# Loading the first modulation columns in two blocks and forming the first eight projection tiles in two halves

## What is computed

```python
c_act = jax.nn.silu(c)
mod = c_act @ w_ada[l] + b_ada[l]
shift1, scale1, gate1, shift2, scale2, gate2 = jnp.split(mod, N_MOD, axis=-1)
h = modulate(rms_norm(x, norm1_g[l]), shift1, scale1)
p = h @ w_in[l]
y_rwkv = rwkv7_mix(p[..., :RWKV_COLS], ...)
y_fox = fox_mix(p[..., RWKV_COLS:], ...)
y = jnp.concatenate([y_rwkv, y_fox], axis=-1) @ w_out[l]
x = x + gate1[:, None, :] * y
h = modulate(rms_norm(x, norm2_g[l]), shift2, scale2)
x = x + gate2[:, None, :] * moe_ffn(h, ...)
```

## Time and profile before

| what | value |
|---|---|
| median of 3 runs | 1242.16 us (1240.57 to 1243.15) |
| span of the profiled execution, first to last instruction | 1237.4 us |
| TensorE matmul, share of the span | 84% |
| VectorE, ScalarE, GpSimd | 26%, 15%, 9% |
| bytes moved | 455.85 MB, 368 GB/s over the span |

### The profile page before, as it was taken

One profiled execution on the slowest core, in us unless ns is written; L12 is line 12 of the kernel. 1 busy time (PEld: TensorE's weight loads), 2 busy tenths in 40 slices (PEclk: granted clock), 3 DMA queues, 4 the chain that ended last, 5 costly groups with the idle time before them and its releaser, 6 DMA issues.

```text
span 1237.4 us, 28436 instructions
## 1 busy us (share of the span) xinstructions
PE 1044.5 (84%) x11067; PEld 523.5 (42%) x11068; DVE 318.7 (26%) x886; ACT 185.3 (15%) x403; POOL 110.2 (9%) x225
## 2 busy tenths in 40 slices
PE   3999999999897999999999796969696969696665
PEld 1777876645342444444444342424242424242222
DVE  0266445448221222222222121212121202121112
ACT  2330224423110111111111010101010101010001
POOL 7020002040000000000000000000010000000000
PEclk9999999999898999999999998889897979898877
DMA  9952236898899939999999999999999999999996
GB/s 367 408 197 67 69 141 233 314 391 306 359 409 424 388 121 430 425 428 427 428 425 430 426 428 427 426 428 426 427 427 429 428 427 428 427 426 428 427 426 285
DMA packets 49521, 455.85 MB, mean 368 GB/s; under 512 B 4790, under 2 KB 5916, under 8 KB 17104
## 3 DMA queue, kind: packets, MB, share of 16 engines
q1 hardware_dynamic: 43152, 417.91, 81.3%
q10 hardware_dynamic: 4960, 33.09, 6.4%
q0 software_dynamic: 1376, 4.38, 1.1%
HBM read 454.29 MB, written 1.07 MB: 368 GB/s over the span
## 4 chain that ended last, share of the span: by engine, by line
PE 50%; DMA 32%; DVE 8%; SPq 4%; issue 2%; ACT 1%; another core or an unknown queue 0%; ACTq 0%; DVEq 0%; POOLq 0%; POOL 0%
DMA raw<-in_w_gate_up 26%; PE bank L2071 19%; PE bank L2085 9%; PE bank L1636 7%; DMA odd<-in_w_gate_up 4%; PE bank L2043 2%; PE bank L1962 2%; SPq L422 2%; PE bank L2094 2%; DMA raw<-in_w_in 1%; DVE aT L1532 1%; DVE gated L1517 1%; DVE ups L1521 1%; SPq L438 1%; DVE ups L1059 1%
## 5 line engine op out<-in xcount | busy, mean ns | idle before, releaser
L2071 PE MATMUL bank<-raw,xT 128*32 128x512 f32 x2176 | 282.2, 665 | 108.3 <-DMA raw<-in_w_gate_up 100.6
L2071 PEld LDWEIGHTS bank<-raw,xT 128*32 128x32 f32 x2176 | 74.6, 117 | 294.9 <-issue 169.3
L1517 DVE TENSOR_TENSOR gated<-bank,bias_i 128x256 f32<-128x256 f32 x51 | 21.6, 424 | 592.9 <-PE bank L2094 592.9
L2085 PE MATMUL bank<-raw,aT 128*32 128x256 f32 x2448 | 142.3, 380 | 10.4 <-DVE aT L1532 10.4
L2071 PE MATMUL bank<-odd,xT 128*32 128x512 f32 x1088 | 131.5, 634 | 20.4 <-DMA odd<-in_w_gate_up 20.3
L962 ACT ACTIVATE evg<-bank 128x512 f32<-128x512 f32 x51 | 30.5, 597 | 689.2 <-PE bank L2071 688.9
L685 POOL TENSOR_TENSOR gatehot<-onehot,gates 128x128 f32<-128x128 f32 x102 | 54.7, 555 | 871.0 <-PE bank L2059 826.8
L1636 PE MATMUL bank<-hT,raw 128*128 128x256 f32 (+1 forms) x496 | 111.3, 382 | 2.1 <-DMA raw<-in_w_in 2.1
L2085 PEld LDWEIGHTS bank<-raw,aT 128*32 128x32 f32 x2448 | 78.1, 110 | 68.7 <-issue 23.8
L1636 PEld LDWEIGHTS bank<-hT,raw 128*128 128x128 f32 (+1 forms) x496 | 91.4, 187 | 19.0 <-issue 3.0
L2071 PEld LDWEIGHTS bank<-odd,xT 128*32 128x32 f32 x1088 | 40.0, 114 | 103.0 <-issue 79.2
(11 more groups left out here) (435 smaller groups left out, 843.5 us busy)
## 6 DMA issues: line engine op xcount, KB each, us to landing
raw<-in_w_gate_up SPq DMA_DIRECT2D x64, 2048.0 KB, 30.1
odd<-in_w_gate_up SPq DMA_DIRECT2D x61, 2048.0 KB, 45.4
dn<-in_w_down SPq DMA_DIRECT2D x16, 2048.0 KB, 47.9
raw<-in_w_down ACTq DMA_DIRECT2D x31, 1024.0 KB, 11.3
raw<-in_w_down SPq DMA_DIRECT2D x15, 2048.0 KB, 39.7
raw<-in_w_down SPq DMA_DIRECT2D x19, 1024.0 KB, 38.5
dn<-in_w_down SPq DMA_DIRECT2D x16, 1024.0 KB, 46.4
raw<-in_w_in SPq DMA_DIRECT2D x7, 2048.0 KB, 16.7
```

The lines of the kernel that those rows point to most:

```text
L1517: body.step("gate", tt(gated[:, :, :, :], turned[:, :, 0:2, :], bias_i[:, :, 0:2].unsqueeze(3).to_broadcast([P, 4, 2, CAP]), ALU.add))
L2071: g = mm(bank[5][j * CAP:(j + 1) * CAP, :], xT[:, u % 2, u // 2, :], gu_slab(u, p)[:, j * NC:(j + 1) * NC], start=u == 0, stop=u == KT - 1)
L2085: g = mm(bank[6][j * CAP:(j + 1) * CAP, 0:NQ], aT[:, k % 4, k // 4, :], dn_slab(u, p)[:, at:at + NQ], start=k == 0, stop=k == KT - 1)
```

## The change

The 2048 columns of shift1 and scale1 are loaded in two blocks. Block 0 holds the columns for slices 0 to 3 of `hT`, block 1 those for slices 4 to 7. Each block is 4 MB, in four groups `g` of two row blocks, each group by two DMAs (shift and scale), with runs of 2 KB instead of 8 KB. Between the blocks SP issues the upper halves (rows for slices 0 to 3) of the first two pieces of `w_in`, and behind block 1 their lower halves. The first eight projection tiles are formed in two halves of four matmuls: two tiles share a bank (banks 7, 5, 0, 1), and ACT evicts a pair only when both are complete. Small rows needed first (`c`, `norm1_g`, `b_ada`: `rows1_in`) are loaded and turned first, and the rest (`rows_in`) later, with a second turn; ten of ACT's small row DMAs and its four lora DMAs move behind its first two `hT` slices. ACT computes the sigmoid of c before the root of the norm, with the tables loaded accordingly.

```diff
-ROWS = [('c', 8), ('norm1_g', 8), ('mu_shift', 14), ... ('b_ada', 16)]
+ROWS = [('c', 8), ('norm1_g', 8), ('b_ada', 16), ('mu_shift', 14), ...]
+NHALF = 8
+HALF_BANK = (7, 5, 0, 1)
...
+        def load_mod(sp, part, g):
+            for h in range(2):
+                sp.dma_start(mod_rows(part, g)[:, :, h, :],
+                             ada_view[:, 2 * g:2 * g + 2, h * D + part * NC:h * D + (part + 1) * NC])\
+                    .then_inc(mod_landed(part, g)[0], 16)
...
-            for k in range(KT):
-                if k == 4:
-                    sp.wait_ge(S("rows_in"), 16 * NROWDMA)
-                sp.dma_start(first_rows[k], ada_view[:, k, 0:2 * D]).then_inc(*ada_landing(k))
+            for g in range(4):
+                load_mod(sp, 0, g)
...
-            for n in range(SRING):
-                load_piece(n)
+            for n in range(2):
+                load_in_half(n, 0, S(f"w_half{n}"))
+            for g in range(4):
+                load_mod(sp, 1, g)
+            for n in range(2):
+                load_in_half(n, 1, S(f"w_loaded{n}"))
+            load_piece(2)
...
+            def turn_half(part):
+                act_e.wait_ge(S("ada_used"), KT * (part + 1))
+                a.activation(first4[:, part * 2 * P:(part + 1) * 2 * P], bank[4][:, 0:2 * P], ACT.Copy)\
+                 .then_inc(S("quarters_ready"), 1)
+                act_e.wait_ge(S("modc_ready"), part + 1)
+                for k in (4 * part, 4 * part + 1):
...
             def take_tile(n):
-                act_e.wait_ge(S("p_mm"), n + 1)
+                act_e.wait_ge(S("p_mm"), n // 2 * 2 + 2 if n < NHALF else n + 1)
...
-            for n in range(3):
+            for n in range(2):
                 take_tile(n)
             act_e.wait_ge(S("shifted"), 1)
...
-            take_tile(3)
-            take_tile(4)
+            for n in range(2, 6):
+                take_tile(n)
             for q in range(6):
                 take_lora(q)
-            take_tile(5)
             take_tile(6)
+            take_tile(7)
             act_e.wait_ge(S("dist_ready"), 1)
             a.activation(e_a[:, :, :], dtmp[:, :, :], ACT.Exp).then_inc(S("exps"), 1)
             a.activation(e_b[:, :, :], dtmp[:, :, :], ACT.Exp, scale=-1.0).then_inc(S("exps"), 1)
-            take_tile(7)
...
+            half_rows(0, 0)
+            half_rows(0, 1)
+            turn_x(0)
+            turn_x(1)
+            half_rows(0, 2)
+            turn_x(2)
+            turn_x(3)
+            half_rows(0, 3)
+            half_turned(0)
...
+            def project_half(n, half):
+                pe.wait_ge(*((S(f"w_half{where_m}"), 16), loaded(where_m))[half])
+                if n == 0:
+                    pe.wait_ge(S("hT_ready"), 2 * half + 2)
+                    pe.wait_ge(S("hT_rest"), 2 * half + 2)
+                for k in range(4 * half, 4 * half + 4):
...
+            for n in range(6):
+                project_half(n, 0)
+            for g in range(3):
+                half_rows(1, g)
+            project_half(6, 0)
+            half_rows(1, 3)
+            project_half(7, 0)
+            half_turned(1)
+            pe.wait_ge(S("rows_in"), 16 * NROWDMA)
+            tr(bank[4][:, 0:NROW], rowv[:, :], ident[0:NROW, 0:NROW]).then_inc(S("rowsT"), 1)
...
-            for n in range(5):
-                project(n)
+            for n in range(6):
+                project_half(n, 1)
+            pe.wait_ge(S("colv_ready"), 2)
             next_rows((0, 1))
...
-            for n in range(5, 10):
-                project(n)
+            project_half(6, 1)
+            project_half(7, 1)
+            project(8)
+            project(9)
             next_rows((2, 3, 4, 5))
```

More of the change, by code:

```diff
@@ L334, in build, with tile_bank @@
         place_of = {m: n for n, m in enumerate(ORDER)}
+        def tile_bank(n):
+            if n < NHALF:
+                return bank[HALF_BANK[n // 2]][:, n % 2 * T:n % 2 * T + T]
+            return bank[n % 2][:, 0:T]
         def used(n):
@@ L721, in _ @@
             act_e.dma_start(bfc[:, :], b_f.rearrange("o h -> h o")).then_inc(S("lora_in"), 16)
[L724 to L739, removed]
+            turn_half(1)
             def take_tile(n):
                 m = ORDER[n]
-                act_e.wait_ge(S("p_mm"), n + 1)
+                act_e.wait_ge(S("p_mm"), n // 2 * 2 + 2 if n < NHALF else n + 1)
                 if m < RT:
-                    i = a.activation(pz[:, m, 1:T + 1], bank[n % 2][:, 0:T], ACT.Copy)
+                    i = a.activation(pz[:, m, 1:T + 1], tile_bank(n), ACT.Copy)
                 elif m < INT - 1:
-                    i = a.activation(pf[:, m - RT, :], bank[n % 2][:, 0:T], ACT.Copy)
+                    i = a.activation(pf[:, m - RT, :], tile_bank(n), ACT.Copy)
                 else:
@@ L1593, in _ @@
             pe.wait_ge(S("consts"), 1)
-            pe.wait_ge(S("rows_in"), 16 * NROWDMA)
-            tr(bank[5][:, 0:NROW], rowv[:, :], ident[0:NROW, 0:NROW]).then_inc(S("rowsT"), 1)
+            pe.wait_ge(S("rows1_in"), 16 * 3)
+            tr(bank[5][:, 0:NROW1], rowv[0:NROW1, :], ident[0:NROW1, 0:NROW1]).then_inc(S("rowsT"), 1)
             def ada_rows(k, rows, b):
@@ L1601, in ada_rows, with half_rows, half_turned @@
                 i.then_inc(S("ada_used"), 1)
+            def half_rows(part, g):
+                pe.wait_ge(*mod_landed(part, g))
+                rows = mod_rows(part, g)
+                for k in range(2):
+                    for q in range(CT):
+                        i = mm(bank[4][q * CAP:(q + 1) * CAP, 0:2 * P], csw[:, 2 * g + k, :],
+                               rows[:, k, q // 2, q % 2 * 2 * P:(q % 2 + 1) * 2 * P],
+                               start=g + k == 0, stop=2 * g + k == KT - 1)
+                    i.then_inc(S("ada_used"), 1)
+            def half_turned(part):
+                pe.wait_ge(S("quarters_ready"), part + 1)
+                if part:
+                    pe.wait_ge(S("modc_ready"), 1)
+                for t in range(2):
+                    at = 8 * part + 4 * t
+                    i = mm(bank[6][:, at:at + 4], first4[:, (2 * part + t) * P:(2 * part + t + 1) * P], ident[:, 0:P:CAP],
+                           start=True, stop=True)
+                i.then_inc(S("col_mm"), 1)
             def turn_x(pair):
@@ L1610, in turn_x @@
                 i.then_inc(S("xnT"), 1)
-            pe.wait_ge(S("csw_ready"), 3)
-            for j in range(4):
-                turn_x(j)
-                for k in (2 * j, 2 * j + 1):
-                    pe.wait_ge(*ada_landed(k, 0))
-                    ada_rows(k, first_rows[k], 4)
-            pe.wait_ge(S("quarters_ready"), 1)
-            for s in range(4):
-                i = mm(bank[6][:, 4 * s:4 * s + 4], first4[:, s * P:(s + 1) * P], ident[:, 0:P:CAP], start=True, stop=True)
-            i.then_inc(S("col_mm"), 1)
+            pe.wait_ge(S("csw_ready"), 1)
+            half_rows(0, 0)
[7 more added lines that the diff above has]
+            half_turned(0)
             def project(n):
@@ L1670, in _ @@
             pe.wait_ge(S("lora_in"), 16 * 4)
+            pe.wait_ge(S("p_ev"), 4)
             for q in range(6):
@@ L2164, in _ @@
             scatter_rest(n_it - 1, True)
-NROWDMA = 17
+NROWDMA = 14
 def kernel(**inputs):
```

130 lines of the change are left out of this document (84 added, 46 removed).

## The result

The changed kernel takes 1249.69 us (median of 18 runs, 1248.11 to 1253.07); the kernel before, run beside it, takes 1243.16 us (18 runs, 1240.57 to 1247.53). The ratio is 1.0046 [1.0037, 1.0056]: slower by 5.7 us by the ratio and by 6.5 between the medians, where 1.1 was forecast, and 1249.69 is outside the range. The profiled execution of the changed kernel took 1250.28 us with a span of 1248.5 us.

The account below looks back on a forecast made before the run. Expert layer limited by weight loads, released by TensorE; ACT and DVE bound 65.5 to 94 us. From `b_f_` at 80.2, 14.8 us of TensorE work gives 95.0 instead of 93.9: +1.1, so 1243.3 us; 8-in-10 range 1239.9 to 1245.8.

Parts of the forecast that it names:

- The start: First modulation sums at 14.1 us: x lands at 5.95, then three groups of block 0 take 8.1 us.
- The first half tile: After block 0's sums and turns end at 21.7 us, 2.8 us to make `hT`, so it starts at 24.5.
- the slow matmuls at TensorE's start: In block 0's sums and turns: 1.4 us lost at TensorE's start, carried over from the earlier trace.
- The second halves: After block 1's turn and its `hT` slices: start at 44.3 us, with no load holding TensorE.
- the clock falls in a gap of the head: Rival: clock falls from 21.7 to 24.5 or 42.6 to 44.3; costs 1.8 us, giving 1245.1 us; chance 0.11.
- From there to the exponentials: From the second halves at 44.3 us to the exponentials at 65.95, exactly as before: 21.65 us.
- what is late next: DVE chain behind the exponentials arrives where it did: `b_f_` at 80.2 us, `kinv` at 93.9.
- The wait at `head_sums`: TensorE reaches `head_sums` at 75.9 us and waits 4.3 us for `b_f_` instead of 0.86.
- the clock behind it: Behind the wait at `head_sums` the clock falls to 1.2 GHz, costing 1.8 us (bounds 0 and 2.3).
- the forecast's 95.0: `back_heads(kinv)` at 95.0 us instead of 93.9, 14.8 us of TensorE work after 80.2.
- the forecast of +1.1: Whole kernel: 1.1 us slower, span 1237.4 to 1238.5, median 1243.3 us; chance 0.50.
- Behind 95 us: After about 95 us TensorE is the bound, its work is untouched, and nothing moves by itself.

Follow-up runs that it names:

- e2: The kernel before with GpSimd's memset of LR waiting until all mid row blocks are used; ratio 0.9985 [0.9973, 0.9997] to the kernel before.
- e3: The kernel before with the four mid row blocks that release the memset issued ahead of tile 9; ratio 1.0065 to the kernel before.
- e7: e2 with ACT's first two exponentials ahead of the evictions of tiles 5 and 6; ratio 0.9995 to the kernel before.
- e10: The changed kernel with ACT's exponentials ahead of the evictions of tiles 6 and 7, memset left in place; ratio 0.9951 to the kernel before.
- e5: e1 with ACT's first two exponentials ahead of the evictions of tiles 6 and 7; ratio 0.9956 to the kernel before.
- e1: The changed kernel with GpSimd's memset of LR waiting until all mid row blocks are used; ratio 0.9994 to the kernel before.
- e6: e5 with 7 filler matmuls in TensorE's waits ahead of the first half tile; ratio 0.9955 to the kernel before.

## Why the prediction was wrong

**The start** was right: first sums at 14.27 us (14.1), no load holds TensorE behind that, and the 387 GB/s of the earlier trace rows was the right rate.

**The first half tile** came at 25.30, not 24.5: the first phase ends at 22.55 (21.7). Most of it is a term that was too small: the slow matmuls at TensorE's start. The first 32 records of the sums take 3.6 us and the eight of the turns behind them 1.6, where the later ones of the same number take 2.0 and 1.0, so 2.2 us are lost where 1.4 was carried over. The granted clock reads 1.00 there, so why they are slow is open.

**The second halves** started at 47.15, not 44.3. This is the sum of 0.8 from above, 1.7 from the clock, 0.5 because a half that stands alone takes 1.99 and not 1.75 us, less 0.2 for the shorter gap. The 1.7 is the rival "the clock falls in a gap of the head", which had 0.11 and a price of 1.8. Its price was right. Its chance was argued from one wait of one execution, the 2.1 us ahead of 34.18 in the earlier trace rows; e2, e3 and e7 show that behind the same place of the kernel before the clock falls too: the five tiles there take 17.53 us in one execution and 20.37 to 20.52 in three others. The Trainium skill, "TensorE: Matmul & The Clock Gate", Part 1, calls the number of slow matmuls at a kernel's start run-variable; these rows agree in kind, behind a wait. Also, if the runs of before contain such executions, a fall in the head is not all extra.

**From there to the exponentials** the term of 21.65 us was right: 68.81 less 47.15 is 21.66.

**The step that failed** is the first sentence of what is late next: "The DVE chain thus arrives where it did: `b_f_` at 80.2". `b_f_` came at 87.8. Of these 7.6 us, 2.85 came with the late second halves, and 4.8 are the memset of `LR`, which no step had. Right dates ahead of it would not have saved the step. With the forecast's own, the memset would start behind the row blocks, at about 76 us, and last to about 83, while `kk_f` would be ready at its old 77.75: by the 0.93 us that the held group ends behind the memset, `b_f_` would come late by an estimated 5 us. I moved TensorE ahead of the DVE chain and asked who waits for TensorE on DVE and ACT, but not on GpSimd, whose queue was not in the reading at all. The sign was in the trace of before, in the row of `a_f` at 7.32 us. The Trainium skill has the rule as well, "SBUF — State Buffer", section "Who interferes with whom": VectorE and GpSimd share one port pair under an exclusive lock, held for a whole instruction, which VectorE takes only in its two-port modes, or for a second SBUF input against a GpSimd instruction that reads SBUF. The rows agree with the rule as far as they go: the memset only writes, and the product with two SBUF inputs runs under it (1.23 us, e10), as does `k_f` (1.67 us in the changed kernel), while the `tensor_scalar` on `kk_f` and on `a_f` is held until it ends. That these are in a two-port mode no row shows. The last part shows too: three `scalar_tensor_tensor` on `r_f` and `k_f` take 2.83 us beside GpSimd's copies to `Td` and `TdT`, which read SBUF (e10, from 93.47), and 1.27 under the memset (e2, from 97.17).

**The wait at `head_sums`** and the clock behind it were right in kind, and both too small. In the changed kernel the wait is 9.35 us (4.3), and `head_sums` and the three tiles take 14.29 where they take 11.27 in e5, 3.0 us lost (1.8). `head_sums` starts 7.7 us later than forecast (87.92) and another 1.3 are lost behind it: together the 9.0 by which `back_heads` misses the forecast's 95.0. In e1, which has no collision, it is 4.58 us (4.3) with 1.6 us lost behind it (12.91 for `head_sums` and three tiles, 11.27 in e5; 1.8 was forecast). `back_heads` is at 97.54 there against 96.91 in e2, and the time is 1.1 us more by the ratios, with intervals that overlap. So without the memset nothing would have spoken against the forecast of +1.1, but that would have been luck: two misses offset each other, the fall in the head, unforeseen after and unseen before.

**Behind 95 us** little moved by itself, as assumed: from `back_heads` to the end of the span are 1143.5 us before and 1144.5 after. But over all twelve profiles this piece is 1142.0 to 1147.3 long, with no order that I can see, and why is open. So a difference between two spans is poor evidence here. The date of `back_heads` is better for what happens ahead of it, but it leaves out this piece, as e5 and e7 show.

## What to carry to other kernels

When a change brings one engine forward or another back, list everything that each of their semaphores releases, on all queues, GpSimd's fills and copies too, and see which instruction of the neighbour it will now lie beside. A group that takes several times what the same operations take elsewhere in the trace is a wait that the busy time hides; find its partner before trusting an order of dates. And read a stretch behind a short wait in more than one profile, since a single execution may show the code at its luckiest.

## What the runs showed of the hardware

- A GpSimd memset of 128x8192 f32 takes 6.92 to 7.01 us and holds a VectorE `tensor_scalar` until it ends (four of them take 5.91 to 7.32 us instead of 1.14). The trace counts VectorE as busy all the while. Operations with two tensor inputs ran under it at their usual length.
- The granted clock fell to 1.2 GHz behind waits as short as 1.52 us (e6's second gap), 1.64 (the changed kernel's first) and 1.74 (e2), and did not behind 1.52 us in the changed kernel's second gap, 1.64 in e5 or 2.1 in before's profile. So the length of the wait alone does not decide it. One fall cost 1.4 us (e3, behind `head_sums`) to 3.0 (e2, first tiles; changed kernel, behind `head_sums`).
- An activation table load takes 1.28 us and the activation behind it starts at once (68.81 to 70.10).
